# Sub-layer seams with three whole first half units, an extra weight tile split in the out phase before, and later modulation steps in two blocks

## The reference

```python
def modulation(cond, w, b):
    m = jax.nn.silu(cond) @ w + b          # w: (1024, 9 * 1024), twice: c and c_ctx
    return m.reshape(cond.shape[0], 1, N_MOD, D_MODEL)
def modulate_in(x, g_pre, mod, j):
    return rmsnorm(x, g_pre) * (1.0 + mod[:, :, 3 * j + 1]) + mod[:, :, 3 * j]
def gated_residual(x, out, g_post, mod, j, weight):
    return x + weight * mod[:, :, 3 * j + 2] * rmsnorm(out, g_post)
def swiglu(h, w13, w2):
    a, g = jnp.split(h @ w13, 2, axis=-1)
    return (jax.nn.silu(g) * a) @ w2
def shortconv_mixer(h, w_in, conv_w, conv_b, w_out):
    gb, gc, xin = jnp.split(h @ w_in, 3, axis=-1)
    return (gb * dwconv_centred(gc * xin, conv_w, conv_b)) @ w_out
```

## Time and profile before

| | |
|---|---|
| median of 3 runs | 2453.85 us (2453.64 to 2454.42) |
| the profiled execution | 2452.03 us, its span 2450.2 us |
| busy PE, DVE, ACT, POOL | 2404.4, 1757.9, 981.3, 436.1 us |
| granted clock of TensorE, mean | 0.998 |
| moved by DMA | 297.96 MB, mean 122 GB/s |

### The profile page before, as it was taken

One profiled execution on the slowest core, in us unless ns is written; L12 is line 12 of the kernel. 1 busy time (PEld: TensorE's weight loads), 2 busy tenths in 40 slices (PEclk: granted clock), 3 DMA queues, 4 the chain that ended last, 5 costly groups with the idle time before them and its releaser, 6 DMA issues. The chain is left out here.

```text
span 2450.2 us, 38986 instructions
## 1 busy us (share of the span) xinstructions
PE 2404.4 (98%) x15173; PEld 2204.5 (90%) x15173; DVE 1757.9 (72%) x2469; ACT 981.3 (40%) x1917; POOL 436.1 (18%) x462
## 2 busy tenths in 40 slices
PE   6999999999999999999999999999999999999998
PEld 6998999889889789979988997998899989989997
DVE  5988785675554679778846878885577759856863
ACT  4442343533445455324434442443511154423432
POOL 1220120201115222102213210220200022201211
PEclk9999999999999999999999999999999999999999
DMA  7526333385212453353252426334154433243333
GB/s 228 164 61 217 94 86 128 115 261 154 54 51 74 108 181 87 125 160 87 78 172 104 131 71 229 87 87 138 52 180 139 135 107 90 71 148 98 87 111 113
DMA packets 347229, 297.96 MB, mean 122 GB/s; under 512 B 38799, under 2 KB 296839, under 8 KB 347047
## 3 DMA queue, kind: packets, MB, share of 16 engines
q1 hardware_dynamic: 341798, 278.64, 37.7%
q0 software_dynamic: 5248, 16.83, 1.8%
HBM read 280.57 MB, written 14.80 MB: 121 GB/s over the span
## 5 line engine op out<-in xcount | busy, mean ns | idle before, releaser
L2013 DVE TENSOR_TENSOR w_lo<-w_raw,w_hi 128x512 fp32r<-128x512 f32 (+1 forms) x249 | 211.4, 852 | 243.6 <-ACT w_hi L1419 242.6
L1419 ACT ACTIVATE w_hi<-w_raw 128x512 fp32r<-128x512 f32 (+1 forms) x249 | 188.3, 760 | 467.1 <-DMA w_raw<-in_ffn_w_dram 201.5
L913 PE MATMUL psum<-w_hi,act_hi 128*128 128x512 f32 x800 | 318.3, 398 | 0.4 <-DVE w_lo L2013 0.4
L915 PE MATMUL psum<-w_hi,act_lo 128*128 128x512 f32 x800 | 317.2, 396 | 0.0
L914 PE MATMUL psum<-w_lo,act_hi 128*128 128x512 f32 x800 | 317.0, 396 | 0.0
L1046 PE MATMUL psum<-hT_hi,w_hi 128*128 128x320 f32 x912 | 281.9, 309 | 0.5 <-DVE z_quarters L2301 0.5
L1048 PE MATMUL psum<-hT_hi,w_lo 128*128 128x320 f32 x912 | 281.8, 309 | 0.0
L1047 PE MATMUL psum<-hT_lo,w_hi 128*128 128x320 f32 x912 | 281.8, 309 | 0.0
L1046 PE MATMUL psum<-t_hi,w_hi_more 128*128 128x320 f32 x608 | 187.9, 309 | 0.0
L1048 PE MATMUL psum<-t_hi,w_lo_more 128*128 128x320 f32 x608 | 187.9, 309 | 0.0
L1047 PE MATMUL psum<-t_lo,w_hi_more 128*128 128x320 f32 x608 | 187.8, 309 | 0.0
(11 more groups left out here) (303 smaller groups left out, 5926.4 us busy)
## 6 DMA issues: line engine op xcount, KB each, us to landing
w_raw<-in_ffn_w_dram SPq DMA_DIRECT2D x96, 512.0 KB, 5.1
w_raw_next<-in_ffn_w_dram SPq DMA_DIRECT2D x80, 512.0 KB, 5.2
w_raw<-in_ffn_w_dram SPq DMA_DIRECT2D x148, 256.0 KB, 3.2
ada_tile_ffn<-in_ada_w_dram SPq DMA_DIRECT2D x56, 512.0 KB, 3.9
ada_direct<-in_ada_w_dram POOLq DMA_DIRECT2D x32, 512.0 KB, 5.7
w_raw<-in_ab_w_in_dram SPq DMA_DIRECT2D x28, 512.0 KB, 4.1
w_raw<-in_sc_w_in_dram SPq DMA_DIRECT2D x24, 512.0 KB, 4.7
ada_tile_sc<-in_ada_w_dram SPq DMA_DIRECT2D x24, 512.0 KB, 3.6
```

The lines of the kernel that those rows point to most:

```text
L913: mm(out, a_hi, b_hi, start=first, stop=False)
L915: return mm(out, a_lo, b_hi, start=False, stop=final)
L1419: A(dst, src, ACT.Copy).then_inc(w_hi_ok, 1)
L2013: V.tensor_tensor(d_, a, b.bitcast(F32), ALU.subtract).then_inc(w_lo_ok, 1)
```

## The change

1. **Seams.** Each seam of s = 1 to 5 computes the first half of units 0 and 1, turns tile 4, computes the first half of unit 2, and then the second halves of units 0, 1 and 2, each in one piece of 320 columns. Unit 2's sums go to PSUM banks 6 and 7 (`THIRD`). The common loop starts at unit 3.
2. **The lead tile.** Unit 0's weights have their own memory (`w_raw_lead`, `w_hi_lead`, `w_lo_lead`). SP loads them (`load_lead`) ahead of the remaining tiles of the out phase of s - 1; ACT and DVE split them (`split_lead`) behind the second half's first tile (u == K), ahead of the next tile. The two common buffers now hold units 1 and 2 over the seam, split where units 0 and 1 were; unit 3 is split once unit 1 is done.
3. **Modulation steps.** `STEPS` is later in ab and sc; `LOADS` stays as it was.
4. Round this: the order of the held and the other tiles at the last token tile of an out phase, the places of `u_pad` and `y_conv`, semaphore counts, a wait of SP on TensorE's unit 0 before one FFN load whose memory the lead overlaps, and a wait of the direct modulation products on the bank of unit 2.

```diff
@@ -83,7 +83,8 @@
 MW, MODC = 256, 1024
-STEPS = {"ffn": [2 + j for j in range(16)], "ab": [1, 1, 2, 2, 3, 3, 4, 4, 5, 6, 7, 9, 10, 10, 11, 11], "sc": [2] + [2 + j for j in range(23)]}
+STEPS = {"ffn": [2 + j for j in range(16)], "ab": [2, 2, 3, 3, 4, 4, 5, 5, 6, 7, 8, 9, 10, 10, 11, 11],
+         "sc": [4, 4, 5, 6, 7, 7, 8, 9, 10, 10] + [11 + j for j in range(14)]}
 SUMS_AT = {"ffn": (10, 18), "ab": (6, 12), "sc": (11, 19, 99)}
...
@@ -251,6 +252,11 @@
+        lead_at = lambda s: arena + 20 * TOK * 4 + HELD[KD] * 4096 if SUBS[s - 1] == "ab" else j0
+        lead_raw = {s: at(f"w_raw_lead{s}", [P, KD, P], lead_at(s)) for s in range(1, len(SUBS))}
+        lead_hi = {s: at(f"w_hi_lead{s}", [P, KD, P], lead_at(s) + 4096, F32R) for s in range(1, len(SUBS))}
+        lead_lo = {s: at(f"w_lo_lead{s}", [P, KD, P], lead_at(s) + 8192, F32R) for s in range(1, len(SUBS))}
+        assert 3 * 4096 <= held_at - j0 and lead_at(2) + 3 * 4096 <= end
...
@@ -704,6 +715,8 @@
                         sp.wait_ge(w_lo_ok, ph["nout"])
+                    if s and not RAW_SLOT[g] and g - ph["g0"] < 2 and not ph["half"]:
+                        sp.wait_ge(pe_unit, ph["nin"] + 1)
                     if g == ph["g0"] and ph["half"] and plan[s][0]["mods"]:
...
@@ -731,6 +744,11 @@
 
+            def load_lead(s):
+                l, f = s // 3, s % 3 // 2
+                w, col = {"ffn": (ffn_w13[l, f], FF), "ab": (ab_w_in[0], COL["qa"]), "sc": (sc_w_in[0], D)}[SUBS[s]]
+                dma(lead_raw[s][:], w.rearrange("(p k) n -> p k n", k=KD)[:, :, col:col + P]).then_inc(lead_loaded, 16)
+
             def reload_x(s, t):
...
@@ -752,13 +770,14 @@
                             load_cols(s + 1)
+                            load_lead(s + 1)
                         for t in range(NT):
...
                         cols = [D, 2 * D, 0, D + P, 2 * D + P, P]
-                        for u in range(SC_IN):
+                        for u in range(1, SC_IN):
                             n = nb + u
...
@@ -931,13 +953,15 @@
 
-            def unit_part(p, h, c0, c1, ready):
+            def unit_part(s, r, h, ready):
+                n = plan[s][0]["nin"] + r
+                out = (THIRD if r == 2 else IN[n % 2])[:, h, 0:HT]
                 for k in range(KD):
...
                         pe.wait_ge(hT_ready, ready[k // (KD // 2)])
-                    hi, lo = w_hi[:, p, k, :], w_lo[:, p, k, :]
+                    hi, lo = (lead_hi[s][:, k, :], lead_lo[s][:, k, :]) if r == 0 else (w_hi[:, n % 2, k, :], w_lo[:, n % 2, k, :])
                     for a, b in ((hi, hT_hi), (hi, hT_lo), (lo, hT_hi)):
-                        last = mm(IN[p][:, h, c0 - h * HT:c1 - h * HT], a, b[:, k, c0:c1],
+                        last = mm(out, a, b[:, k, h * HT:(h + 1) * HT],
                                   start=(k == 0 and a is hi and b is hT_hi), stop=(k == KD - 1 and a is lo))
...
@@ -974,17 +998,18 @@
                 pe.wait_ge(out_evac, ph["oe"] - NT + 3)
-                h0, h3, h4 = [HM(s, 2)] * 2, [HM(s, 3)] * 2, [HM(s, NT - 1), HM(s, NT)]
-                for r, h, c0, c1, ready in ((0, 0, 0, HT, h0), (1, 0, 0, HT, h0),
-                                            (0, 1, HT, 4 * P, h3), (0, 1, 4 * P, TOK, h4), (1, 1, HT, TOK, h4)):
-                    n = ph["nin"] + r
-                    if s and r == 0 and c0 == HT:
-                        turn_x(s, NT - 1)
-                    pe.wait_ge(w_lo_ok, n + 1)
-                    need(pe, in_evac[n % 2], inv(ph, n) - 1)
-                    last = unit_part(n % 2, h, c0, c1, ready)
-                    if c1 == TOK:
-                        last.then_inc(pe_unit, 1)
+                for h in range(2):
+                    for r in range(3):
+                        n = ph["nin"] + r
+                        if h == 0 and r == 2:
+                            turn_x(s, NT - 1)
+                            pe.wait_ge(hmod_ok, HM(s, 3))
+                        pe.wait_ge(*((w_lo_ok, n + 1) if r else (lead_lo_ok, LEAD_LO(s))))
+                        if r < 2:
+                            need(pe, in_evac[n % 2], inv(ph, n) - 1)
+                        last = unit_part(s, r, h, [HM(s, NT - 1), HM(s, NT)] if h else [HM(s, 2)] * 2)
+                        if h:
+                            last.then_inc(pe_unit, 1)
 
...
@@ -1523,6 +1554,8 @@
                     split(ph["nout"] + u, shape="out", u=u, prod=slot_done(ph, u) if seven(ph) and u < 4 else 0)
+                    if final and u == K and s + 1 < len(SUBS):
+                        split_lead(s + 1)
                     for i in range(ph["held"]):
...
@@ -2012,6 +2053,10 @@
 
+            def split_lead(s):
+                dve.wait_ge(lead_hi_ok, LEAD_HI(s))
+                V.tensor_tensor(lead_lo[s][:], lead_raw[s][:], lead_hi[s][:].bitcast(F32), ALU.subtract).then_inc(lead_lo_ok, 1)
+
             def split_held(s, ph, i):
...
@@ -2149,12 +2194,12 @@
                         if q == NT - 1:
-                            split(n + 1)
+                            split(n + 2)
                         add_out(s - 1, q)
...
                         if q == 3:
-                            split(n)
+                            split(n + 1)
                         if q == NT - 1:
...
@@ -2407,25 +2458,30 @@
                             modulate_at(ph, u + 1)
-                        split(n + 2, i, 6)
+                        if not (first(i) and jj == 0):
+                            split(n + 2, i, 6)
                         dve.wait_ge(pe_unit, n + 2 + i * 6)
...
                         ins.then_inc(in_evac[(n + 1) % 2], 1)
+                        if first(i) and jj == 0:
+                            split(n + 3)
                         modulate_at(ph, u + 2)
...
                         own.link(V.scalar_tensor_tensor(yconv[:], upad[:, 2:TOK + 3], col(cw[:, 2, :]), yconv[:], ALU.mult, ALU.add))
-                        split(n + 3, i, 6, shape="out" if last and jj == 1 else None)
+                        if not (first(i) and jj == 0):
+                            split(n + 3, i, 6, shape="out" if last and jj == 1 else None)
                         modulate_at(ph, u + 3)
...
                             off = 0 if t0 < LAT else 1
-                            ins = V.tensor_tensor(ut[:, t0:t1], IN_V[n % 2][:, h, f0:f0 + t1 - t0], yconv[:, t0 + off:t1 + off], ALU.mult)
+                            src = THIRD_V if first(i) and jj == 0 else IN_V[n % 2]
+                            ins = V.tensor_tensor(ut[:, t0:t1], src[:, h, f0:f0 + t1 - t0], yconv[:, t0 + off:t1 + off], ALU.mult)
                         ins.then_inc(in_evac[n % 2], 1)
```

83 lines of the change are left out of this document (55 added, 28 removed).

## The result

The changed kernel takes 2466.84 us (median of 5 runs, 2465.56 to 2470.33) against 2453.85 (5 runs, 2453.46 to 2454.42): ratio 1.0052, 95% interval 1.0041 to 1.0063. It is 13.0 us slower. Forecast were 2458.9 us and a range up to 2464; the sign was right, the size was not.

The account below looks back on a forecast made before the run. TensorE was taken as the bound, busy 2404.4 of 2450.2 us. Seams -2.25 each (s = 1, 2, 3, 5), sc +10.4, ab's out phase +2.9 and sc's +0.8 sum to +5.1; forecast 2458.9 us, eight-in-ten range 2451 to 2464.

Parts of the forecast that it names:

- The seams, -2.25 each: In five seams, one 320-column piece replaces unit 0's 192- and 128-column pieces: 5.83 - 3.58 = 2.25 us less each.
- sc: SP is held: At sc's start, loads waiting for late steps hold the weight tiles behind them: +10.4 us, the seam's gain included.
- The granted clock is 1.00 in the windows and is no part of the sum.: Whole kernel: TensorE's clock taken at full speed as in the profile before, with no time counted for it.
- The lead in ab's out phase, +2.9: In ab's out phase, the lead's 1.75 us of queue and 1.15 on VectorE delay the last products: +2.9 (1.5 to 4).
- sc's out phase, +0.8: In sc's out phase, the lead makes the last held tile's low part late: +0.8 us (0 to 2).
- The FFN out phases, 0 each: In the three FFN out phases, no tile waits noticeably, so the lead costs 0, with 2.9 as bound for each.
- SP isn't held: The first rival: sc keeps only unit 3's wait, -1.9 for s = 4 in place of +10.4, 2446.6 us; chance 0.15.
- The lead isn't hidden in the FFNs either: Rival for the three FFN out phases: 2.9 us each, +8.7, 2467.6 us, half of it 2463; chance 0.12.

Follow-up runs that it names:

- Experiment 4: The kernel before with nothing but the late STEPS of sc: 2464.50 us, ratio 1.0045.
- experiment 2: The changed kernel with sc's LOADS one unit later for steps 3 to 7, its late STEPS kept: 2451.40 us, ratio 0.9995.
- Experiment 7: Experiment 5 with the load of step 5 back at unit 5, so that unit 6's weight tile is held once: 2454.07 us, ratio 0.9994.
- experiment 8: The kernel before with unit 0's second half in one piece in every seam, no lead and no third half unit: 2465.23 us, ratio 1.0044.
- experiment 5: Experiment 2 with sc's first three loads and the small bias rows moved from behind unit 2's weight tile to behind unit 4's: 2448.47 us, ratio 0.9975.
- experiment 10: Experiment 9, but behind ab the lead is loaded ahead of the out tiles again, its split staying late: 2444.91 us, ratio 0.9956.
- experiments 3: The changed kernel with every lead loaded behind the last out tile and split behind the seam's first token tile: 2460.35 us, ratio 1.0028.
- 6: Experiment 5 with the lead loaded and split late for the seam behind ab alone: 2445.74 us, ratio 0.9964.
- 9: Experiment 5 with the lead of every seam loaded behind the last out tile and split behind the first token tile: 2442.14 us, ratio 0.9950.
- 1: The changed kernel with STEPS of sc as before the change, all else kept: 2456.13 us, ratio 1.0022.
- 11: The changed kernel itself run once more, against the kernel before: 2466.26 us, ratio 1.0048.

## Why the prediction was wrong

The sum had +5.1 us and the traces part by 14.8. By the table the 9.7 between them are sc 4.6, the three FFN out phases 3.4, the start 1.1, sc's out phase 0.9, ab's out phase and the end 0.6, the seams -0.8. Two steps of the prediction failed: it put the granted clock at nothing, and the lead in the FFN out phases at nothing. The order of its terms, their places and most of their sizes held.

- *The seams, -2.25 each.* Right in size: -2.27, then -2.5 three times. Their working holds a misreading: the 3.13 us of the 192-column piece contain the wait of 0.21 and the gap about it. Its matmuls follow each other at 114 ns, not 130, nearly as fast as those of 128 columns (113). So some 1.9 us of the 2.25 are matmul time and some 0.4 are the wait, which was in the sum already. The 0.2 more in the other seams comes with the halves and the unit behind them: 147 to 148 ns a matmul, where the common units before took 149; in s = 1 they took 147 in both. The gap rule of the Trainium skill ("TensorE: Matmul & The Clock Gate", section "Back-to-back issue gap"), by which the seams would give nothing, is not borne out: the estimate by it is 56, 82.5 and 136 ns for 128, 192 and 320 columns.
- *sc: SP is held.* Right in place, order and chain: TensorE waited 13.0 us there (forecast 14.3), one step's end to the next unit took 7.7 us (7.6). Experiment 4 has the hold with the late steps alone, experiment 2 takes it away with the loads alone. Two sizes were off: unit 3's own wait is 2.92 (forecast 1.9), since its tile landed 1.1 us later, and unit 8's chain took 9.2.
- *"The granted clock is 1.00 in the windows and is no part of the sum."* This is the first step that failed. It was true of the kernel before in that stretch and was carried over to a kernel with waits of 3 to 4 us. In sc the clock fell three times, 5.9 us of TensorE's work. Experiment 7 shows it from one hold, experiment 8 in another place without any hold, and with no waits (experiment 5) it is at 1.00 throughout that stretch. The 5.9 us did not all reach the end: where the next unit was held anyway, the slow unit ate into its wait (0.43 and 1.84 us at units 7 and 5, forecast 2.8 and 3.2). sc came out at +15.0 where the sum had +10.4. Of these 4.6, by the starts of the units, some 3 are the later tiles of units 3 and 8, and 1.7 the clock behind unit 8. The waits and the clock can't be added as if each stood alone.
- *The same window, before and changed*, 1765 to 1865, for the whole of it at one glance:

```profile
1765.00:1865.00 100.00, 98.04 (x683) 1.00 0.46 143
```

```profile
1765.00:1865.00 100.00, 86.82 (x549) 0.93 0.41 122
```

- *The lead in ab's out phase, +2.9.* Measured +3.2, and this is luck in part: the tiles waited less than forecast (2.8 us in all, before 0.6), and the clock made up for it. TensorE's two last tiles and the window about them:

```profile
839.80 0.50 PE L935 MATMUL psum<-w_hi,mix_act 128*128 128x512 f32 x1 [1.84 <-DVE w_lo L2054]
...
841.29 0.80 PE L935 MATMUL psum<-w_hi,mix_act 128*128 128x512 f32 x1 [0.44 <-DVE w_lo L2054]
```

```profile
840.00:843.50 3.50, 3.06 (x8) 0.57 0.16 47
```

  3.50 x 0.43 = 1.5 us are the clock's. Of the split of the cost, 1.75 for the queue and 1.15 for VectorE's order, experiment 10 supports the first (1.6 to 2.5 us) and gives no sign of the second, as the tiles wait no longer with the split than without it. The 1.75 itself rests on 300 GB/s for a fully used queue, and the window in experiment 5 has 418 GB/s at a share of 1.02.
- *sc's out phase, +0.8.* +1.7 here, one wait of 1.38 on the held tile as described; +0.4 to +1.9 in the kernels with an early lead, 0 in those without. In experiments 3 and 5 to 7 another 1.3 to 1.6 are lost in the seam behind it. That is the clock, which falls there for 3.4 us in each of these four and in the changed kernel doesn't.
- *The FFN out phases, 0 each.* This is the second step that failed: +0.5, +1.1 and +1.7 here. The prediction looked for waits of the tiles, and they did not wait. TensorE waits for the first turn's `part`, 1.36 us (before 0.23) and 2.06 us behind s = 2 and 3. Before and changed, behind s = 3:

```profile
1738.14 1.16 PE L931 MATMUL psum<-ident,part 128*128 128x128 f32 x8 [0.33 <-DVE part L2056]
```

```profile
1738.49 1.16 PE L953 MATMUL psum<-ident,part 128*128 128x128 f32 x8 [2.06 <-DVE part L2101]
```

  TensorE comes to this turn 1.4 us earlier than before, the `part` 0.35 us later. The timelines show how the lead gets there. The last `w_lo` ahead of the sums of the first column half starts 0.40 us later (1722.21 and 1722.61). VectorE's five sums, GpSimd's five products with the gate (together some 10 us), the row's norm and `part` follow it with the same 0.35 to 0.40. In six other profiles with an early lead the stretch up to behind the turn of s = 3 cost -0.3 to +2.6 us (the largest with a fall of the clock in it), in five profiles without it -0.6 to -0.3. So that the lead is the cause is shown for s = 3 (experiments 3 and 9 besides). For s = 2 the scatter without a lead is as wide (-0.5 to +0.7).
- *The start.* +1.1 us before anything that the change touches. The kernel before with late steps (experiment 4) has +1.3 there. It is scatter: the granted clock is at 0.5 for 3.4 or 6.8 us around 25 to 32 us, and the two profiles fell on different sides.
- *Which of them took the time out of the range.* It ended 2.8 us above it. By this trace the clock behind unit 8 and in ab is 3.2 us (1.7 and 1.5), the FFN out phases are 3.4. Taking away the one or the other would have brought the time into the range, so neither can be named alone.
- *The rivals.* "SP isn't held" is refuted. "The lead isn't hidden in the FFNs either" was right by less than half (3.4 of 8.7). The first rival's saving is nevertheless to be had: experiment 5 gets it by moving loads, and 9 ends 12 us under the kernel before.

## What to carry to other kernels

When work is moved later, look for what waits on it in a queue that issues in order: here a table of step places was moved and the table of loads that wait for the steps was not, and each load held the weight tile behind it. Moving the loads by one place turned a loss of 13 us into none, and with the queue's order put right, too, into a gain. The same goes for a queue that waits for something small, as SP did at the bias rows. And when a wait of some microseconds is put on TensorE, price the clock behind it as well, from a stretch in which the engine has such a wait.

## What the hardware showed beyond this

- A fall of the granted clock has one of two sizes: it stays at 0.5 for 3.4 or 6.8 us. Summed over windows of 1 us in sc, the share missing from full speed is 3.41 us for experiments 2 and 7, 5.1 for 1 and 4, 6.8 for 3, 11 and the changed kernel, 0 for 5 and 6: multiples of 1.7.
- In sc's in phase it fell behind every wait for a `w_lo` of 2.7 to 4.5 us (fifteen in seven profiles) and behind none of those of 0.4 to 1.8 alone. Elsewhere the line isn't as clean. Behind the 2.87 of experiment 8 it fell four times in five. In the changed kernel's ab it fell at 840.5, behind waits of 0.50 and 1.84 us. In the seams into s = 2 and s = 5 TensorE waits 0.5, 1.6 and 0.8 us around the turns in every kernel, and the clock fell there in four of thirteen profiles each, at a cost of 1.3 to 1.6 us. What decides between them stays open.
- In seven of the thirteen profiles it fell once inside ab, near 585 us, with TensorE not waiting at all in that stretch (idle 0.0 us in 570 to 600), the kernel before among them. This is some 1.7 us of scatter that has nothing to do with any edit. What sets it off there stays open.
